# First layer of a two-layer decoder: the first sequence's tiles loaded at once, and a second value, query and key projection put into the opening stage

## The reference, cut to what matters

```python
def mixer_sublayer(x, g_pre, g_post, w_in, w_br_dil, w_br_moba, w_out):
    h = rms_norm(x, g_pre)
    proj = h @ w_in   # (B, S, PROJ_COLS)
    qa, ka, va, qb, kb, vb, gate_a, gate_b = jnp.split(proj, PROJ_SPLITS, axis=-1)
...
    for g, (window, dilation) in enumerate(DIL_GROUPS):   # (128,1), (512,4), (2048,16)
        sl = slice(g * DIL_HEADS_PER_GROUP, (g + 1) * DIL_HEADS_PER_GROUP)
        o, lse = dilated_attention(qa[:, :, sl], ka[:, :, sl], va[:, :, sl], window, dilation, slopes[sl])
...
    o_b = moba_attention(qb, kb, vb, slopes[DIL_HEADS:])
    merged = jax.nn.sigmoid(gate_a) * y_a + jax.nn.sigmoid(gate_b) * y_b
    return x + rms_norm(merged @ w_out, g_post)

def reference(x, ...):
    for l in range(DEPTH):                 # 2
        x = mixer_sublayer(x, ...)
        x = ffn_sublayer(x, ...)
    return x
```

## Time and profile before

| what | value |
|---|---|
| median of 3 runs | 4423.77 us |
| the three runs | 4560.96, 3996.86, 4423.77 us |
| profiled execution, its own time | 3906.2 us |
| its span on the slowest core (core 3) | 3904.9 us |
| spans of the 8 cores | 3892.4 to 3904.9 us |
| mean granted TensorE clock of the cores | 0.991 to 0.994 |
| PE busy on core 3 | 3765.8 us, 96% |
| opening stage, core 3 | 0 to about 80.6 us |
| dilated units (0,0) and (1,0), core 3 | about 80.6 to 117.3 and 117.3 to 154.3 us |

### The profile page before, as it was taken

One profiled execution on the slowest core, in us unless ns is written; L12 is line 12 of the kernel. 1 busy time (PEld: TensorE's weight loads), 2 busy tenths in 40 slices (PEclk: granted clock), 3 DMA queues, 4 the chain that ended last, 5 costly groups with the idle time before them and its releaser, 6 DMA issues.

```text
span 3904.9 us, 56082 instructions; the slowest of 8 cores (3892.4 to 3904.9 us)
## 1 busy us (share of the span) xinstructions
PE 3765.8 (96%) x19760; PEld 1810.6 (46%) x19760; DVE 2078.2 (53%) x3265; ACT 1762.5 (45%) x3541; POOL 877.7 (22%) x1484
## 2 busy tenths in 40 slices
PE   6989999999998999999999899999999989999999
PEld 4544444444553444444465344444446534444444
DVE  4454566464346466646434646654643554675463
ACT  3456345253345635535334653552533465354251
POOL 2331232111132133211113213321111322331110
PEclk9999999999999999999999999999999999999999
DMA  6133789454313489875632259994442225797341
GB/s 147 29 72 51 153 173 169 112 97 90 81 32 65 60 165 177 149 171 79 129 79 53 48 77 167 158 156 124 77 105 52 53 47 92 161 179 133 103 71 70
DMA packets 303867, 410.37 MB, mean 105 GB/s; under 512 B 150560, under 2 KB 167200, under 8 KB 303584
## 3 DMA queue, kind: packets, MB, share of 16 engines
q0 software_dynamic: 118656, 190.89, 33.3%
q1 hardware_dynamic: 184944, 215.88, 21.6%
HBM read 500.52 MB, written 67.63 MB: 145 GB/s over the span
## 4 chain that ended last, share of the span: by engine, by line
PE 91%; DVE 4%; ACT 2%; DMA 1%; issue 1%; POOL 0%; SPq 0%; ACTq 0%; POOLq 0%; DVEq 0%
PE psum L383 55%; PE psum L1242 16%; PE psum L538 5%; PE psum L606 5%; PE psum L656 5%; PE psum L935 3%; PE psum L681 2%; ACT s_arena L943 1%; DMA s_xr<-x 1%; DVE s_arena L777 1%; DVE s_arena L694 1%; DVE s_arena L375 1%; ACT s_tz L372 0%; SPq L175 0%; DVE s_hb L460 0%
## 5 line engine op out<-in xcount | busy, mean ns | idle before, releaser
L383 PE MATMUL psum<-s_hT,s_slabs 128*128 128x512 bf16 x9728 | 2180.4, 380 | 12.3 <-DVE s_arena L1203 9.2
L383 PEld LDWEIGHTS psum<-s_hT,s_slabs 128*128 128x128 bf16 x9728 | 940.2, 98 | 1115.7 <-issue 32.1
L1242 PE MATMUL psum<-s_arena 128*128 128x512 bf16 x2816 | 609.1, 379 | 0.0
L1192 DVE SCALAR_TENSOR_TENSOR s_arena<-s_arena,s_convw 128x512 f32<-128x512 f32 x352 | 264.3, 751 | 425.9 <-ACT s_arena L1184 425.8
L1242 PEld LDWEIGHTS psum<-s_arena 128*128 128x128 bf16 x2816 | 275.6, 98 | 332.2
L656 PE MATMUL psum<-s_arena 128*128 128x128 bf16 (+2 forms) x1840 | 354.3, 268 | 63.7 <-DVE s_arena L947 21.5
L420 DVE SCALAR_TENSOR_TENSOR s_tz<-psum,s_stat,s_gpost 128x1024 f32<-128x1024 f32 x128 | 164.1, 1282 | 381.1 <-POOL s_stat L399 381.1
L411 ACT ACTIVATE s_hb<-psum 128x1024 bf16<-128x1024 f32 x128 | 131.0, 1023 | 502.2 <-PE psum L1242 344.0
L943 ACT ACTIVATE s_arena<-psum 128x512 bf16<-128x512 f32 (+3 forms) x640 | 296.1, 547 | 72.5 <-PE psum L935 61.1
L180 POOL DMA_DIRECT2D s_slabs<-w_in_r x224 | 122.5, 550 | 905.8 <-PE psum L656 453.6
L694 DVE TENSOR_TENSOR s_arena<-s_arena,s_dmask 128x512 bf16<-128x512 bf16 (+1 forms) x384 | 192.0, 504 | 217.9 <-ACT s_arena L689 216.2
(11 more groups left out here) (71 smaller groups left out, 3278.9 us busy)
## 6 DMA issues: line engine op xcount, KB each, us to landing
s_slabs<-w_in_r POOLq DMA_DIRECT2D x224, 256.0 KB, 4.8
xs<-s_xr SPq DMA_DIRECT2D x96, 512.0 KB, 3.9
s_xr<-xs SPq DMA_DIRECT2D x96, 512.0 KB, 5.2
s_slabs<-w_gate_r POOLq DMA_DIRECT2D x176, 256.0 KB, 4.6
s_slabs<-w_up_r POOLq DMA_DIRECT2D x176, 256.0 KB, 5.7
s_xr<-x SPq DMA_DIRECT2D x64, 512.0 KB, 6.4
s_arena<-w_down POOLq DMA_DIRECT2D x88, 256.0 KB, 7.3
y<-s_xr SPq DMA_DIRECT2D x32, 512.0 KB, 2.9
```

Of the source, the lines that this page charges most:

```text
L383: inst = nc.tensor.matmul(out, lhsT=l_, rhs=r_, start=(i == 0), stop=(i == n - 1))
L1192: d1 = DVE.do(nc.vector.scalar_tensor_tensor(out=t1_, in0=a_[:, 1 + 512 * tgi:513 + 512 * tgi], scalar=convw[:, l, fc, 1:2], in1=t1_, op0= ...
L1242: inst = nc.tensor.matmul(ps[zb + n], lhsT=uT[:, kc, i * 128:(i + 1) * 128], rhs=wdn[kc][:, n * 512:(n + 1) * 512], start=(kc == 0), stop= ...
```

## The change

- Loads: the opening stage issues the loads of all 16 tiles of x at once. Tiles 0 to 3 go to `xr`, tiles 4 to 15 into twelve homes in `arena` that no one uses yet. The first tile's load stands ahead of that of the gain. The four constants (`convw`, `dmask`, `tri`, `pastc`) are issued behind them.
- Norms: three more buffers for normalised tiles (`hx`, in `arena`) and 8 instead of 4 slots for the sums let `norms` run ahead: ahead of the transposes of tile j it calls the norms up to tile j + 1 + min(4, j//2).
- Order in a step: step j does norms, transposes of tile j, and value chunk j of group 0 right behind them. The copy to `hT` alternates between ACT (even tiles) and DVE (odd tiles).
- Added work: from step 4 on each step also has a value chunk of group 1, a group of four tiles behind, and steps 5, 9, 13, 17 and 7, 11, 15, 19 a query and a key chunk of group 1. Steps 16 to 19 hold only the rest of these.
- `mixer` leaves out of unit (0,0) the projections of group 1, and moves the value projection of group 2 from unit (1,0) into unit (0,0). The queries and keys of group 2 stay in unit (1,0).

```diff
@@ stage_b1, stage_b2, stage_c: h_view / x_view @@
+        hx = [carve(o * KB, 512, BF16) for o in (86, 100, 102)]
...
@@ mixer @@
-                vt[0], qt[(0, 0)] = pre
+                vt[0], vt[1], qt[(0, 0)], qt[(1, 0)] = pre
...
-                    if sp == 0 and g2 > 0:
-                        fills.append(v_proj(l, g2, FB_, vt[g2], p_wait))
+                    gv = i + 1 if pre is None else i + 2
+                    if sp == 0 and gv < 3:
+                        fills.append(v_proj(l, gv, FB_, vt[gv], p_wait))
                         total += 14.4
...
+                    if (g2, sp2) not in qt:
...
@@ opening stage @@
-        for t in range(16 + 2):
-            if t < 16:
-                u = {"t": t, "nx": x0[t]}
-                stage_b1(u)
-                stage_b2(u)
-                if t + NX < 16:
-                    x0.append(x_load(x_src(0, True, t + NX, None)))
...
-            if 1 <= t <= 16:
-                stage_c(first[t - 1], TB_, DVE)
-            if t >= 2:
-                next(v0)
-                if (t - 2) % 4 == 3:
-                    next(qk0)
+        def norms(n):
+            while len(first) < min(n, 16):
+                t = len(first)
+                u = {"t": t, "nx": x0[t], "hs": t % AH, "so": t % NST}
+                stage_b1(u)
+                stage_b2(u)
+                if t in (1, 3, 5):
+                    slab_ring.prefetch(t + 3)
+                first.append(u)
+        for j in range(16 + 4):
+            norms(j + 2 + min(4, j // 2))
+            if j < 16:
+                stage_c(first[j], TB_, (ACT, DVE)[j % 2])
+                next(v0)
+            if j >= 4:
+                next(v1)
+                if j % 4 == 1:
+                    one_tg(qk1[0])
+            if j % 4 == 3:
+                if j < 16:
+                    one_tg(qk0[0])
+                    one_tg(qk0[1])
+                if j >= 4:
+                    one_tg(qk1[1])
```

More of the change, by code:

```diff
@@ L450, in stage_b1 @@
             ACT.wait(tok, hfree[hs], st.get(("stat", so)))
-            ts = ACT.do(nc.scalar.activation(out=hb[:, hs, :], in_=xr[:, sl, :], func=AF.Square, accum_out=stat[:, 1, so, 0:1]))
+            ts = ACT.do(nc.scalar.activation(out=h_view(hs), in_=x_view(sl), func=AF.Square, accum_out=stat[:, 1, so, 0:1]))
             u["b_tok"] = (sl, tok, ts, rms_scale(1, so, ts))
@@ L459, in stage_b2 @@
             DVE.wait(tr, ts, tok, gtok[1])
-            th = DVE.do(nc.vector.scalar_tensor_tensor(out=hb[:, hs, :], in0=xr[:, sl, :], scalar=stat[:, 1, so, 2:3], in1=gpre[:, :],
+            th = DVE.do(nc.vector.scalar_tensor_tensor(out=h_view(hs), in0=x_view(sl), scalar=stat[:, 1, so, 2:3], in1=gpre[:, :],
                                                        op0=ALU.mult, op1=ALU.mult))
@@ L479, in stage_c @@
             for c in range(8):
[L480 removed]
+                inst = nc.tensor.transpose(out=pb[:, c * 128:(c + 1) * 128], in_=h_view(hs)[:, c * 128:(c + 1) * 128], identity=identb[:, :])
             tp = PE.do(inst)
@@ L584, in load_w, with v_proj @@
             return slab_ring.load((l, "in", ci))
-        def v_proj(l, G, banks, toks, waits):
+        def v_proj(l, G, banks, toks, waits, t_ones=None, taus=range(16)):
             V = Vb[G]
-            t_ones = ones_memset(V, waits)
+            if t_ones is None:
+                t_ones = ones_memset(V, waits)
             c0 = 12 + 2 * G if G < 3 else 22
@@ L595, in v_proj @@
             tp = None
-            for tau in range(16):
+            for tau in taus:
                 r = (128 * tau) // L
@@ L1269, in ffn @@
                 load_gain(1, (l + 1) % n_layers, 2)
+        AH = NH + len(hx)
+        hfree += [[] for _ in hx]
+        homes = [12 + 4 * i for i in range(6)] + [52 + 4 * i for i in range(6)]
+        x0_so = [SemObj(nc, es, f"x0_{i}") for i in range(len(homes))]
+        x0 = [x_load(x_src(0, True, 0, None))]
         load_gain(1, 0, 0)
-        first = []
+        slab_ring.prefetch(2)
+        ones0 = ones_memset(Vb[0], [])
+        ones1 = ones_memset(Vb[1], [])
         t_hb = DVE.do(nc.vector.memset(halfb[:, :], -0.5))
@@ L1291, in build @@
-        qk0 = qk_tg()
-        CT = None
-        for t in range(16 + 2):
-            if t < 16:
-                u = {"t": t, "nx": x0[t]}
+        for t in range(1, 16):
+            if t < NX:
+                x0.append(x_load(x_src(0, True, t, None)))
+            else:
+                xa = carve(homes[t - NX] * KB, 1024)
+                x0.append((xa, dma(SP, xa, x_src(0, True, t, None), x0_so[t - NX])))
+        dma(SP, convw[:, :, :, :].rearrange("p a b c -> p (a b c)"), convw_d[:, :], c_so)
@@ new lines, in build @@
+        dma(SP, dmask[:, :, :].rearrange("p a b -> p (a b)"), dmask_d[:, :], c_so)
+        dma(SP, tri[:, :], tri_d[:, :], c_so)
+        CT = dma(SP, pastc[:, :, :].rearrange("p a b -> p (a b)"), pastc_d[:, :], c_so)
+        PE.wait(ID)
+        vt0, vt1, qt0, qt1 = [], [], [], []
+        v0 = v_proj(0, 0, ALL6, vt0, [], ones0)
+        v1 = v_proj(0, 1, ALL6, vt1, [], ones1, [4 * r + m for m in range(4) for r in range(4)])
+        qk0 = [qk_one(0, 0, 0, w, QK[0], [], qt0, ALL6) for w in range(2)]
@@ L1296, in build, with one_tg @@
+        qk1 = [qk_one(0, 1, 0, w, QK[1], [], qt1, ALL6) for w in range(2)]
+        def one_tg(gen):
+            for _ in range(1):
+                next(gen)
+        first = []
+        def norms(n):
+            while len(first) < min(n, 16):
+                t = len(first)
+                u = {"t": t, "nx": x0[t], "hs": t % AH, "so": t % NST}
                 stage_b1(u)
                 stage_b2(u)
-                if t + NX < 16:
-                    x0.append(x_load(x_src(0, True, t + NX, None)))
@@ L1318, in build @@
+        for gen in [v0, v1] + qk0 + qk1:
+            drain(gen)
         load_gain(0, 0, 1)
@@ L1322, in build @@
         outs = []
-        p_wait = []
+        p_wait = [first[15]["h_tok"]]
         for s in range(n_seq):
@@ L1326, in build @@
             for l in range(n_layers):
-                rest, r_free = mixer(s, l, xs_tok, p_wait, (vt0, qt0) if s == 0 and l == 0 else None)
+                rest, r_free = mixer(s, l, xs_tok, p_wait, (vt0, vt1, qt0, qt1) if s == 0 and l == 0 else None)
                 ffn(s, l, xs_tok, rest, r_free)
```

40 lines of the change are left out of this document (10 added, 30 removed).

## The result

| | before | changed |
|---|---|---|
| median of 7 runs | 4118.57 us | 3924.38 us |
| lowest run | 3901.15 us | 3923.21 us |
| ratio of the undisturbed runs | | 1.0054, 95% interval 1.0033 to 1.0076 |
| profiled execution's span | 3904.9 us | 3922.1 us |
| mean span of the 8 cores | 3897.0 us | 3917.8 us |

In some executions of either kernel all cores of a die run slower at a lower granted clock; the medians above contain such executions, while the ratio, all profiles and every time called undisturbed leave them out. The change makes the kernel 0.5% slower, some 21 us, inside 2% but clear of no change.

The account below looks back on a forecast made before the run. PE, busy 96% of the span, was taken as the bound, so only idle time could move. The second unit ends at 124 + 73.7 - 29.3 + 5 = 173.4 against 154.3 us: 3906.2 + 19 = 3925 us, range 3895 to 4445.

Parts of the forecast that it names:

- The main term: Opening stage: PE idle waiting for copies to hT, 21.6 us for tiles 4 to 10.
- The units: Units (0,0) and (1,0): 29.3 us less of their 73.7 us, plus 5 us of waits from thinner filling.
- The loads: Opening stage: issuing all x loads at once gains 2 us at the first tile and nothing more.
- The order of the queues as cause: ACT and DVE queues are strict FIFO; if engines took what is ready, the sum would be 14.2 us less.
- Tiles 0 to 3 ... I take 35: Opening stage: these tiles end at 35 us (33 to 39) against 34.0 before; 2 us won, some 3 lost.
- The clock term: Opening stage behind tile 3: 4 us lost to the lower PE clock, bounds 0 and 10.
- The upper end of 4445: Top of the time range, from the before median: 4424 + 19 = 4443; the change's own range was 3895 to 3945.
- 0.93 on no change: Whole kernel: chance of "same", since every case lay between -0.4% and +1.0%; faster 0.03, slower 0.04.
- That the norms get out of the way: Rival, opening stage: ACT and DVE finish a step's norms while PE still works, 3902 or 3890 us; chance 0.12.
- The clock rival: Opening stage: PE works at 1.2 GHz from tile 3 to tile 10, 3946 us; chance 0.12.
- The loads did not choke: Rival, opening stage: a core's loads get under 130 GB/s; at 100 GB/s 18 us more, 3943; chance 0.04.
- No effect: Rival, whole kernel: 3906 us, needing gains at the first tiles that cancel 19 us; chance 0.04.

Follow-up runs that it names:

- the run with late loads: The change with x tiles again loaded through four slots of xr and the constants behind tile 9's norm: 3917.9 to 3923.4 us, ratio 1.0046.
- chunks later: The change with all projection chunks one step later, chunks of step j-1 behind the transposes of tile j: 3889.8 to 3891.2 us, ratio 0.9966.
- copy first: The change with the norms called behind the transposes and the copy to hT, value chunk still right behind: 3903.3 to 3908.2 us, ratio 1.0007.
- all ACT: The change with all copies to hT on ScalarE instead of alternating: 3909.6 to 3913.3 us, ratio 1.0024.
- all DVE: The change with all copies to hT on VectorE instead of alternating: 3939.0 to 3941.4 us, ratio 1.0098.

## Why the prediction was right or wrong

**The mechanism held.** The main term was 21.6 us of idle for tiles 4 to 10 and 5.0 for tiles 11 to 15; measured 20.7 and 5.1 (0.87 + 1.24 + 0.88 + 1.19 + 0.88), tile by tile within 0.4 us. (Two slips of working changed nothing: the terms of tiles 5 and 9 give 4.3 and not 4.2, and 12 x 0.52 + 6 x 0.26 is 7.8.) The units: forecast 49.4 us for both (73.7 - 29.3 + 5), measured 50.2, with 3.3 + 0.7 us of waits in place of the 5. The loads: forecast nothing beyond the first tile, 2 us; the first transposes came at 13.5 instead of 16.35 us, 2.9 earlier, ACT waited for x only at the first three tiles (12.8 us), and the run with late loads shows no other value. The copy on ACT, priced at 1.06 from another operation, took 1.00. The order of the queues as cause was argued in the prediction; the runs show it from four sides (chunks later, copy first, all ACT, all DVE).

**What was mis-sized.** "Tiles 0 to 3 ... I take 35", with "some 3 lost to the copies": they ended at 39.2 us on the slowest core, at the edge of the stated bounds (33 to 39), and at 37.0 on core 3, from which the sum was made. The copies cost 2.5 to 2.8 us at each of the four tiles, 10.7 us of waits in all where 3 were allowed, and the clock of 16 to 34 us was 0.70 where it had been 1.00. This is the whole miss in the stage's end, 128.3 instead of 124. The clock term behind it held: from tile 4's transposes to the first scores the slowest core took 128.34 - 39.19 = 89.15 us, of which PE was busy 63.4 for 58.6 us of work at full price, a loss of 4.8 where 4 was taken, and idle 25.7 where 26.6 was forecast. The forecast of this part was 89.2.

The core matters: the slowest core after is core 7, whose first scores came before at 84.7 us, and not core 3 with its 80.6. By the mean of the 8 cores' spans the change costs 20.9 us, by the profiled slowest cores 17.2, by the undisturbed runs about 21; the forecast was 19. That 3925 meets the measured 3924.4 within 1 us is partly luck: the 19 us were added to 3906.2, some 3 us more than the kernel before takes undisturbed (3901.2 and 3904.7), and the effect was 2 us too small.

**What was wrong.** The step from the sum to a forecast of two medians. "The likeliest single value is the one with the profile's conditions, 3925" was set beside a kernel before at 4423.77 us. Taken together the two say 11% faster, and the mechanism said 0.5% slower. The spread of the three runs was left without a price ("nothing in the profile prices this"), although the profiled execution, 3906.2, was already below all three. The runs showed that the median given for the kernel before is no measure of the kernel: of seven runs each, the kernel before has a median of 4118.57 and a lowest of 3901.15, the changed one 3924.38 and 3923.21, and the ratio is 1.0054, the 0.5% of the mechanism. The upper end of 4445, taken from "4424 + 19", was not needed; the 3895 to 3945 beside it was the range to give.

The same section has a second wrong step, "within the 2% that a measurement of this kernel can tell from no change", and with it 0.93 on no change. Five of the seven runs lie between 3923.2 and 3925.7 us, and the ratio's interval (1.0033 to 1.0076) leaves no change out. A forecast of +19 us should have said that this is a slowdown which can be measured.

**The rivals.** That the norms get out of the way, 3890 to 3902, is what the kernel with later chunks does (3890.8), not the change. The clock rival did not come: from 40 to 92 us the clock was 0.84, above the 0.75 at which it was to decide, and against the kernel before only 3.8 us of busy time were lost instead of 25. The loads did not choke: from 16 to 34 us they ran at 288 GB/s. "No effect" would have needed gains of 19 us at the first tiles; there were 3.

## What to carry to other kernels

To run ahead in the numbering of tiles is not to run ahead on the engines: write down, for each engine, what stands between an instruction that PE waits for and the moment its input is ready. Work for later tiles belongs behind the copy that the next matmul needs, and a matmul belongs one step behind the copy it reads; dropping that one-step distance cost more (33 us with the clock) than all that early loads, far norms and added work gave. When a stage is bound by such a loop, price the lost clock beside the idle time: here each us of idle time added or taken away moved PE's busy time by 0.2 to 0.6 us the same way. And put before and after on the same footing: a time worked out from a profiled execution belongs beside the time of that execution, not beside a median of runs that scatter by hundreds of us.

## What the runs showed of the hardware that was not expected

- The clock moved with the waits and added to them. Over 34 to 95 us it was 0.84 in the change, 0.82 with all copies on VectorE, 0.89 on ScalarE, 0.94 with the copy first and 0.97 with later chunks; the trace has only stretches at 2.4 and at 1.2 GHz, and these are their means. PE's busy time moved by 2 to 9 us with 8 to 23 us of idle time.
- With many large DMAs queued, issuing one more took SP longer. Before, one issue took about 0.45 us (four constants at 46.5 to 47.9 us). With all of x being queued:

```profile
11.48 12.59 SPq L180 DMA_DIRECT2D s_arena<-x  x5
```

12.59 us for five issues, while the DMA engines were busy nearly all the time (share 0.85 up to 16.35 us, 1.02 behind); the four constants behind them went out from 24.1 us on and took 1.1 to 3.0 us each. That the full queues are the reason is not shown by a run of its own. Nothing waited for the constants here.
- A copy of 128 x 1024 bf16 from PSUM to SBUF took 1.00 us on ACT and 0.68 on DVE.
